# Expert blocks written out without loops, a two-pass block's rows twice in the slots, in the order heavy, two two-pass, two heavy, two two-pass, heavy

## The reference

```
logits = xt @ router_w                       # 256 tokens, 8 experts
top_v, top_e = lax.top_k(logits, 2)
gate = softmax(top_v)
# the assignments are sorted by expert and packed in blocks of 128 rows
yb = (silu(xblk @ w1[e]) * (xblk @ w3[e])) @ w2[e]     # w1, w3: 1024x3584, w2: 3584x1024
y  = segment_sum(yb * slot_w, slot_tok)                # back to the tokens
```

## Time and profile before

| | |
|---|---|
| median of 3 runs | 2000.74 us (1996.06 to 2002.03) |
| the profiled execution's own time | 2004.05 us |
| span of the profiled execution | 2002.3 us |
| PE busy | 1900.4 us, 95% of the span |
| DVE busy | 1626.4 us, 81% |
| ACT busy | 1295.0 us, 65% |
| mean granted PE clock | 0.991 |
| time between the first and the last product of the expert blocks | 1018.4 to 1990.8 us |

### The profile page before, as it was taken

One profiled execution on the slowest core, in us unless ns is written; L12 is line 12 of the kernel. 1 busy time (PEld: TensorE's weight loads), 2 busy tenths in 40 slices (PEclk: granted clock), 3 DMA queues, 4 the chain that ended last, 5 costly groups with the idle time before them and its releaser, 6 DMA issues.

```text
span 2002.3 us, 31226 instructions
## 1 busy us (share of the span) xinstructions
PE 1900.4 (95%) x11849; PEld 1682.8 (84%) x11849; DVE 1626.4 (81%) x1726; ACT 1295.0 (65%) x1221; POOL 44.6 (2%) x98
## 2 busy tenths in 40 slices
PE   8999999999999999999999988899889998788898
PEld 8999999989999999999988766687667876666686
DVE  6998966577778988876478988789887898888886
ACT  7666555344336656554467777777777787777675
POOL 0000000000000000000000000000000000000000
PEclk9999999999999999999999999999999999999999
DMA  8545555455554645564489999999999999999994
GB/s 261 175 132 189 167 172 190 141 168 190 190 181 156 190 128 174 168 222 155 161 295 373 362 391 394 326 374 362 394 389 329 375 361 394 367 365 396 325 389 171
DMA packets 311162, 532.78 MB, mean 266 GB/s; under 512 B 14362, under 2 KB 157362, under 8 KB 311014
## 3 DMA queue, kind: packets, MB, share of 16 engines
q1 hardware_dynamic: 308550, 523.71, 74.2%
q0 software_dynamic: 2464, 7.03, 1.3%
HBM read 526.30 MB, written 6.29 MB: 266 GB/s over the span
## 4 chain that ended last, share of the span: by engine, by line
PE 64%; DVE 17%; issue 8%; ACT 6%; DMA 4%; SPq 1%; DVEq 0%; ACTq 0%
PE ps L2047 18%; PE ps L2049 17%; PE ps L2048 17%; DVE w_lo L1302 12%; PE ps L2362 4%; ACT w_hi L807 4%; DMA raw<-in_moe_w 3%; PE ps L2364 2%; ACT w_hi L800 1%; PE ps L2572 1%; DVE c L1369 1%; PE ps L2216 1%; PE ps L2236 1%; PE ps L2573 1%; PE ps L2466 1%
## 5 line engine op out<-in xcount | busy, mean ns | idle before, releaser
L1302 DVE TENSOR_TENSOR w_lo<-raw,w_hi 128x2048 fp32r<-128x2048 f32 (+1 forms) x330 | 741.8, 2259 | 185.2 <-ACT w_hi L800 130.8
L2047 PE MATMUL ps<-a_hi,w_hi 128*128 128x256 f32 x1456 | 416.2, 286 | 2.0 <-DVE a_lo L1657 1.6
L2048 PE MATMUL ps<-a_lo,w_hi 128*128 128x256 f32 x1456 | 411.9, 283 | 0.0
L2049 PE MATMUL ps<-a_hi,w_lo 128*128 128x256 f32 x1456 | 411.8, 283 | 0.0
L807 ACT ACTIVATE w_hi<-raw 128x2048 fp32r<-128x2048 f32 x168 | 321.6, 1918 | 100.4 <-PE ps L2049 68.5
L800 ACT ACTIVATE w_hi<-raw 128x2048 fp32r<-128x2048 f32 x157 | 296.2, 1894 | 57.2 <-PE ps L2049 52.0
L2047 PE MATMUL ps<-w_hi,a_hi 128*128 128x512 f32 (+1 forms) x800 | 306.5, 383 | 20.7 <-DVE w_lo L1302 17.6
L2049 PE MATMUL ps<-w_hi,a_lo 128*128 128x512 f32 (+1 forms) x800 | 301.3, 377 | 0.0
L2048 PE MATMUL ps<-w_lo,a_hi 128*128 128x512 f32 (+1 forms) x800 | 301.3, 377 | 0.0
L2047 PEld LDWEIGHTS ps<-a_hi,w_hi 128*128 128x128 f32 x1456 | 278.9, 192 | 3.7 <-issue 2.0
L2048 PEld LDWEIGHTS ps<-a_lo,w_hi 128*128 128x128 f32 x1456 | 279.0, 192 | 0.4
(11 more groups left out here) (394 smaller groups left out, 3116.7 us busy)
## 6 DMA issues: line engine op xcount, KB each, us to landing
raw<-in_moe_w SPq DMA_DIRECT2D x168, 1024.0 KB, 7.6
raw<-in_w_in SPq DMA_DIRECT2D x66, 1024.0 KB, 5.2
mem_t<-in_moe_w SPq DMA_DIRECT2D x56, 1024.0 KB, 7.7
area<-in_moe_w SPq DMA_DIRECT2D x56, 1024.0 KB, 7.6
xf<-in_moe_w SPq DMA_DIRECT2D x56, 1024.0 KB, 7.5
raw<-in_ffn_w SPq DMA_DIRECT2D x33, 1024.0 KB, 5.3
raw<-in_w_mlstm_out SPq DMA_DIRECT2D x8, 1024.0 KB, 4.9
raw<-in_w_out SPq DMA_DIRECT2D x8, 1024.0 KB, 6.0
```

The lines of the kernel that those rows point to most:

```text
L1302: return dve.tensor_tensor(dst, whole, as_f32(hi), ALU.subtract)
L2047: pe.matmul(dst, wh, xh, start=start, stop=False, skip_group_check=True)
L2048: pe.matmul(dst, wh, xl, start=False, stop=False, skip_group_check=True)
L2049: return pe.matmul(dst, wl, xh, start=False, stop=stop, skip_group_check=True)
```

## The change

1. All blocks are written out; there is no loop on any engine up to block 7. The kinds become "HLLHHLLH".
2. A light block's rows stand twice in the 128 slots (`iota_pair` counts 0 to 63 twice, and `select` uses it for a light block). So both halves of its output rows have the gate of their own row and an address in memory: the output is scaled straight out of the banks, as for a heavy block (ACT the lower 512 columns, DVE the upper), and POOL adds the two halves of the rows to `h_sums` with two transfers, one after the other. `y_low` and its additions go.
3. With the kind of the next block known at each place, only the one layout of the gathered rows that it needs is made (before, the last light block of each loop turn made both).
4. The hidden step of a light block is spread over two posts: silu and "gated" stay after the second w1 chunk, the high and the low half move to the post of the chunk behind it (`L_HALVES_AT`). For the last group both stay together.
5. `plan` is cut in two and moved from ahead of block 0 into the posts of its chunks 2 and 5.

```diff
-KINDS = "HLHLHLLH"
+KINDS = "HLLHHLLH"
...
+L_SILU_AT = {E_AT["w1", n + 1, 1]: n for n in range(NGE - 1)} | {E_AT[TURN_LAST]: NGE - 1}
+L_HALVES_AT = {E_AT["w3", n + 1, 0]: n for n in range(NGE - 1)} | {E_AT[TURN_LAST]: NGE - 1}
...
-            with sp.Fori(1, NE - 1) as b:
+            for b in range(1, NE - 1):
...
+            pool.iota(iota_pair, pattern=[[0, 2], [1, LIGHT]], base=0, ...)
...
-                pool.indirect_dma_start(out=h_sums, ... add_row[0:n, 0:1] ..., in_=y_rows[0:n, :], ...).then_inc(y_added.sem, 16)
-                pool.wait_ge(y_added.sem, y_added.at(b, 16))
+                for r in (slice(0, LIGHT), slice(LIGHT, P)) if KINDS[b] == "L" else (slice(0, P),):
+                    pool.indirect_dma_start(out=h_sums, ... add_row[0:r.stop - r.start, 0:1] ..., in_=y_rows[r, :], ...).then_inc(y_added, 16)
+                    parts += 1
+                    pool.wait_ge(y_added, 16 * parts)
                 pool.sem_inc(added.sem, 1)
...
             def l_post(...):                                   # ACT
                 if m == N_EXP - 1:
-                    for n, done in enumerate((y_half.at(b, 1), None)):
...
-                        act.activation(y_low[:, n * 512:(n + 1) * 512], ps[4 + n][LIGHT:P, :], ACT.Copy).then_inc(l_copied.sem, 1)
-                    for n in range(2):
-                        c = slice(n * 512, (n + 1) * 512)
-                        act.wait_ge(l_y_sum.sem, l_y_sum.at(j, n + 1))
-                        act.activation(y_rows[0:LIGHT, c], y_low[:, c], ACT.Copy, scale=gate_col[0:LIGHT, :]).then_inc(ye_done.sem, 1)
+                    act.wait_ge(y_half.sem, y_half.at(b, 1))
+                    act.activation(y_rows[:, 0:512], ps[4][:, :], ACT.Copy, scale=gate_col).then_inc(ye_done.sem, 1)
...
-                if m in turned:
-                    n = turned[m]
+                if m in L_SILU_AT:
+                    n = L_SILU_AT[m]
                     act.wait_ge(e_turned.sem, e_turned.at(b, n + 1))
                     act.activation(act_l[n % 2], ps[6][:, 0:T], ACT.Silu).then_inc(e_silu.sem, 1)
+                if m in L_HALVES_AT:
+                    n = L_HALVES_AT[m]
                     act.wait_ge(e_gated.sem, e_gated.at(b, n + 1))
                     act.activation(hid_both[n % 2][:, :, 0, :], ...).then_inc(e_hid_hi.sem, 1)
...
-            with act.Fori(0, N_PAIRS) as i:
-                e_block(2 * i)
-                l_block(2 * i + 1, i, "HL")
-            l_block(NE - 2, N_PAIRS, "H")
+            for b in range(NE - 1):
+                if KINDS[b] == "L":
+                    l_block(b, LIGHT_NO[b], KINDS[b + 1])
+                else:
+                    e_block(b, False, KINDS[b + 1])
...
             def e_post(b, m, last=False, following="L"):       # DVE
+                if not last and b == 0 and m == 2:
+                    plan_order()
+                if not last and b == 0 and m == 5:
+                    plan_tables()
...
             def l_post(...):                                   # DVE
+                dve.wait_ge(e_pe.sem, e_pe.at(b, m + 1))
                 if m == N_EXP - 1:
-                    for n in range(2):
...
-                        dve.tensor_tensor(y_low[:, c], y_low[:, c], ps[4 + n][0:LIGHT, :], ALU.add).then_inc(l_y_sum.sem, 1)
+                    dve.tensor_scalar(y_rows[:, 512:D], ps[5][:, :], gate_col, None, ALU.mult).then_inc(ye_done.sem, 1)
                     return
```

More of the change, by code:

```diff
@@ L81 @@
 LIGHT = 64
-KINDS = "HLHLHLLH"
+KINDS = "HLLHHLLH"
 N_LIGHT = KINDS.count("L")
-N_PAIRS = 3
+LIGHT_NO = [KINDS[:b].count("L") for b in range(NE)]
 N_OVER = 4
@@ L286, in trunk @@
         before = flat2(k_t)[:, D:D + P]
[L287 removed]
+        iota_slot, iota_pair = (flat2(k_t)[:, D + i * P:D + (i + 1) * P] for i in (1, 2))
         vflat = vx[:, :, :, :].rearrange("p a b c -> p (a b c)")
@@ L1156, in gather_hi, with e_post @@
                     ins.then_inc(x_hi_done.sem, 1)
-            def e_post(b, m, last=False):
+            def e_post(b, m, last=False, following="L"):
                 kind, g, i = ESEQ[m]
@@ L1197, in e_block @@
                     if first:
-                        e_post(b, t - SPL, last)
+                        e_post(b, t - SPL, last, following)
                     if t < N_EXP:
@@ L1903, in over_halves, with plan_order @@
                 return t.rearrange("p (o e) -> p o e", o=1).broadcast_to([P, TT, NE])
-            def plan():
+            def plan_order():
                 ch.link(dve.tensor_copy(total, ps[5][:, 32:32 + NE]))
@@ L1996, in _ @@
             slot_rows(0, ps[5][:, 64:67])
-            plan()
             def tail(b):
@@ L2015, in tail @@
                     dve.tensor_scalar(f_tile[0][:, c], f_tile[0][:, c], f_stat[3][:, 0:1], None, ALU.mult).then_inc(f_out.sem, 1)
-            with dve.Fori(0, N_PAIRS) as i:
-                e_block(2 * i)
-                l_block(2 * i + 1, i, "HL")
-            l_block(NE - 2, N_PAIRS, "H")
+            for b in range(NE - 1):
+                if KINDS[b] == "L":
+                    l_block(b, LIGHT_NO[b], KINDS[b + 1])
+                else:
+                    e_block(b, False, KINDS[b + 1])
             further_blocks()
@@ L2619, in tail @@
                         pe.matmul(dst, s, y_lo_e[:, c], start=False, stop=True, skip_group_check=True).then_inc(f_mul.sem, 1)
-            with pe.Fori(0, N_PAIRS) as i:
-                e_block(2 * i)
-                l_block(2 * i + 1, i)
-            l_block(NE - 2, N_PAIRS)
+            for b in range(NE - 1):
+                if KINDS[b] == "L":
+                    l_block(b, LIGHT_NO[b])
+                else:
+                    e_block(b)
             e_block(NE - 1, True)
```

75 lines of the change are left out of this document (32 added, 43 removed).

## The result

The changed kernel takes 2011.71 us in the median of 7 runs (2007.44 to 2017.41), the kernel before beside it 2000.51 us (7 runs, 1994.15 to 2005.14). The ratio is 1.0057 with a 95% interval of [1.0043, 1.0071]: slower by 0.6%, where 2017.6 us and a range of 1987 to 2030 were predicted. The profiled execution is the fastest of the seven, 2007.44 us, with a span of 2005.6 us and a mean granted clock of 0.990.

What follows compares the result with a forecast made beforehand. It took DVE with the hidden step to bound light rounds, PE heavy ones, plus slow joins. Terms -27.1 - 1.5 + 19.2 + 26.3 = +16.9 on 2000.74 us gave 2017.6 us, range 1987 to 2030.

Steps and rivals of the forecast that it cites:

- Joins, -27.1: Where a light block hands over to the next: excess waiting falls from 36.6 to 9.5 us, a gain of 27.1.
- The correction of 3.3: The profiled execution lay 3.3 us above the median of the runs, so the forecast was lowered from 2021.0 to 2017.6.
- The plan, -1.5: Moving plan into block 0 ends PE's wait of 1.47 us: gain 1.5, or 0 without slack on DVE.
- POOL's two additions in a row stay hidden: Two output-row additions end some 15 us after outputs are ready, asked for 26 us into the block: cost 0.
- The 6.2 that stayed at the join 6-7: Light-heavy join 6-7: only the output chain's wait of about 3.1 of 9.3 us goes, as further blocks' tables stay on DVE.
- The ring, +19.2: Light blocks: late low half and three buffer pairs close a PE, ACT, DVE wait cycle of 16.82 us; 24 rounds, +0.8 each.
- The clock, +26.3: PE's 2.8 us pause before the first w2 chunk halves its clock in seven of eight of 24 light rounds, 1.25 us each.
- seven of eight rounds: Share of light rounds expected to lose the clock, from eight PE waits of 1.95 us or more in the expert blocks.
- The rule against it: The Trainium skill ties clock falls to idle gaps longer than expected here: clock term 0, time 1991.3 us; the forecast followed the trace.
- The first (clock whole, 1991.3): Light rounds: the cycle of waits is there but the clock holds, removing 26.3 us; 1991.3 us, chance 0.22.
- The second (no ring, 1972.1): Light rounds stay at the transfers' 16.0 us, leaving only the gains of joins and plan; 1972.1 us, chance 0.14.
- The third: Written-out code pays the loop's 3.1 us again at joins 1-2, 2-3 and 3-4; 2027 us, chance 0.05.

Runs made afterwards that it cites:

- the kernel with the halves back: The changed kernel with only part 4 undone, so high and low half stand again after the second w1 chunk; 1978.7 us, ratio 0.989.
- the filled pause: The changed kernel plus 18 small unused transposes on PE in each pause ahead of a light block's first w2 chunk; 1997.2 us, ratio 0.9983.

## Why the prediction was right, and where it was off

The sum was -27.1 - 1.5 + 19.2 + 26.3 = +16.9; the runs give -21.7 + 18.5 + 14.5 = +11.3. The forecast's mechanism, shorter joins against a ring and the clock's falls in its pause, holds. The term that missed most is the clock, 11.8 us too large; the gain of joins and plan, 6.9 us too large the other way, hid over half of it. That the total came within 6 us is in part this luck.

- *Joins, -27.1.* By the profile this was right. Taking off the undisturbed 15.05 and 16.8, the excess of the joins that leave a light block is now 1.0, 1.3, 1.0 and 4.4, together 7.8 us, where 9.5 was predicted and 36.6 stood before. By the medians the kernel with the halves back gains only 21.7. The profiled executions differ by 2004.05 - 1975.02 = 29.0; one lies 3.7 above its median of 2000.38, the other 3.7 below. A sum read from one execution of before carries that execution's clock falls at its joins; that this is where the 7 us went is likely, but was not shown. The correction of 3.3 in the prediction took off the level, but left the gain at its full size.
- *The plan, -1.5.* The wait of 1.47 us ahead of the fourth chunk of block 0 is gone, but DVE's new instructions in the post of chunk 2 delay its next splits and "gated", and PE waits for that:

```profile
1035.10 0.66 PE L2464 MATMUL ps<-ident,z_sig 128*128 128x128 f32 x4 [1.15 <-DVE z_sig L1833]
```

The first six chunks of block 0 take 18.50 us in place of 18.55. That is the prediction's lower case, "without that slack, 0". An earlier start of block 0 can't be told: it lies at 1018.1 to 1018.4 in the three profiles with the plan ahead of it, and at 1016.7 to 1018.9 in the nine without.
- *Where the joins' gain is from.* The loop and the rest are shown apart: the loops 7.7 us, rows twice with the single layout and the plan 13.1, the order nothing that can be told. How the 13.1 divide was not tried. That POOL's two additions in a row stay hidden fits: no wait of PE, ACT or DVE in the expert blocks names POOL. The 6.2 that stayed at the join 6-7 was 4.4, and more than half of it goes with the tables.
- *The ring, +19.2.* Measured 18.5 by the medians; by the two profiles the four light blocks are longer by 20.6 us, 16.0 of it in the twenty rounds from w2 to w2 (17.1 against 16.3, 0.8 each as predicted) and 4.6 at entries and ends. Work added to it came out in full. But the 0.8 has two misses in it that cancel, which is luck: the ring is 17.13 and not 16.82, and the rounds that it replaces are 16.2 to 16.3 in the mean and not 16.04, which was read from two of them. The 0.3 is spread over the links, each longer by 0.08 us at most than in the rows that I took (the first 2.18 for 2.13, the last from the low half to PE 0.56 for 0.48). The same ring takes 16.87 inside a loop, so most of this goes with the written-out code; what it is there was not settled.
- *The clock, +26.3.* This is the term that was mis-sized: the filled pause shows 14.5 us. The predicted pause of 2.8 us was 2.99. But "seven of eight rounds" lose the clock was drawn from eight waits at joins, and in the profiled execution it was 11 of 24. It lies 10.2 us above the 1997.2 of the filled pause, so that a loss cost 0.9 in the mean (in the dearest round 18.64 less 17.13, 1.5), where 1.25 was taken: 11 x 0.9 in place of 21 x 1.25. The profiled execution is the fastest of the seven. For the slower ones the mean clock allows an estimate: eleven falls of 3.4 us and the half clock at the very end make the 0.990 of the profiled execution, so 0.987 in the median run stands for some 14 falls and 0.981 in the slowest for some 21. By that the 14.5 us are 1.0 us for each fall. What decides in which round a pause of 2.99 us costs the clock stays open: blocks 2 and 5 lost it in their last three rounds, block 1 in its first two, block 6 in its first three, and but for the first of block 1 the pauses are alike. In all eleven the half clock began between 0.1 us ahead of the pause's end and 1.5 us behind it.
- *The rule against it.* Pauses of 2.99 us cost 14.5 us here, so following the trace was right, with a larger share than it was worth. The Trainium skill (TensorE: Matmul & The Clock Gate, "HAM oscillation — how this bites in real kernels") ties the fall to gaps longer than these, the 3.85 us at block 1 excepted, and by it the term would be near 0. The trace does not agree: the clock fell at ten pauses of 2.95 to 3.01 us, though thirteen such pauses cost nothing. Those of 4.4 to 5.1 us in the kernel with only DVE's half late always did.
- *The rivals.* The first (clock whole, 1991.3) is the kernel with the filled pause, 1997.2. The second (no ring, 1972.1) is the one with the halves back, 1978.7. Both are 6 to 7 us above what I gave, by the same shortfall in the joins. The third, written-out code paying at block starts, is refuted: no join shows 3 us of unexplained idle time. Written-out code pays only the 0.24 us in a round of the ring.

## What to carry to other kernels

When an operation is moved behind another one in an engine's list to spare that engine a wait, follow the thing it produces: if its consumer stands early in the next engine's list and the buffers are few, the delay closes a ring, and the round gets longer although every engine has idle time. Judge each engine's share of such a move apart, since here DVE's late half cost 35 us beside ACT's and 98 without it (35.5 and 97.8 by the medians), while ACT's late half alone cost nothing. A join between stages is read cheaply from its own windows, but the gain should be set against several executions. And small work in a pause that cannot be avoided gives back what the clock takes (14.5 us here), though removing the pause was worth more.

## What the runs showed of the hardware

- Pauses of equal length don't cost equally: of 24 pauses of PE, all but one some 3 us long, 11 brought half clock for 3.4 us, while those of 4.4 to 5.1 us did in all 24 rounds, mostly for 6.8 us. In the kernel with the filled pause 24 pauses of some 1 us brought none. Executions of the same kernel then differ by 10 us (2007.44 at a mean clock of 0.990, 2017.41 at 0.981), where the kernel with the filled pause, at 0.996 to 0.999, has 12 within 5.6 us.
- A hardware loop's jump cost ACT 3.10 us without work, with a table load of 1.28 us behind; written out both vanish, and the joins concerned lose 5.2 us. The same code costs 0.24 us more in a ring of some seven hand-overs when written out (17.11 against 16.87 us); the cause is open.
- At 394 GB/s ACT waits for the 1 MB chunks of a light round, at some 16 us for six, in the kernel with only ACT's half late: the next bound once the engines are out of the way.
